# Long convolution of a two-layer kernel: a transform over 256 frequencies replaced by one over 128, with sums and differences on VectorE

## The reference

```python
def _bidir_long_conv(u, filt, bias):
    """y[t] = sum_s u[s] h(t - s) over offsets -(L-1)..(L-1), via FFT with zero padding to 2L. u: (B, L, C)."""
    l, ch = u.shape[1], u.shape[2]
    kern = jnp.concatenate([filt[:, :ch], jnp.zeros((1, ch), filt.dtype), filt[:0:-1, ch:]], axis=0)
    kern = kern * lax.rsqrt(jnp.sum(kern * kern, axis=0, keepdims=True))
    spec = jnp.fft.rfft(u, n=2 * l, axis=1) * jnp.fft.rfft(kern, axis=0)[None]
    y = jnp.fft.irfft(spec, n=2 * l, axis=1)[:, :l]
    return y + u * bias

def _hyena_mixer(p, ...):
    p = _short_conv(p.astype(f32), conv_w.astype(f32), conv_b.astype(f32))
    v, x1, x0 = jnp.split(p, 3, axis=-1)
    filt = _implicit_filter(...)
    return x0 * _bidir_long_conv(x1 * v, filt, bias.astype(f32))
```

## Time and profile before

| | |
|---|---|
| median of 3 runs | 3259.18 us |
| the profiled execution | 3258.49 us, span 3256.7 us |
| PE busy | 3151.7 us, 97% of the span |
| PEld busy | 2882.9 us, 89% |
| DVE busy | 1973.1 us, 61% |
| ACT busy | 1604.5 us, 49% |
| POOL busy | 2030.5 us, 62% |
| granted TensorE clock | 0.99 of full speed, mean |

### The profile page before, as it was taken

One profiled execution on the slowest core, in us unless ns is written; L12 is line 12 of the kernel. 1 busy time (PEld: TensorE's weight loads), 2 busy tenths in 40 slices (PEclk: granted clock), 3 DMA queues, 4 the chain that ended last, 5 costly groups with the idle time before them and its releaser, 6 DMA issues.

```text
span 3256.7 us, 59652 instructions
## 1 busy us (share of the span) xinstructions
PE 3151.7 (97%) x21316; PEld 2882.9 (89%) x21316; DVE 1973.1 (61%) x3192; ACT 1604.5 (49%) x2377; POOL 2030.5 (62%) x2676
## 2 busy tenths in 40 slices
PE   7999999999999999999998999999999999999998
PEld 7999999999888888888866989999987888888887
DVE  6566665666678766775866884555554443434344
ACT  6455554555454434444434665556554434444443
POOL 5777777777556655665643467888764555555553
PEclk9999999999999999999998999999999999999999
DMA  7676666666675575575545777676665555555553
GB/s 237 212 236 224 216 223 212 230 222 217 243 251 188 191 239 182 182 234 193 188 144 175 252 266 240 209 230 216 213 237 161 185 184 187 188 181 191 184 188 116
DMA packets 262849, 672.99 MB, mean 207 GB/s; under 512 B 28311, under 2 KB 65912, under 8 KB 262008
## 3 DMA queue, kind: packets, MB, share of 16 engines
q1 hardware_dynamic: 262584, 669.55, 62.6%
HBM read 663.12 MB, written 6.32 MB: 206 GB/s over the span
## 4 chain that ended last, share of the span: by engine, by line
PE 79%; POOL 8%; DVE 6%; issue 4%; DMA 2%; ACT 2%; SPq 0%; DVEq 0%; POOLq 0%; ACTq 0%
PE psum L768 30%; PE psum L769 15%; POOL w_lo L590 8%; PE psum L761 7%; PE psum L763 7%; PE psum L762 7%; PE psum L766 2%; PE psum L1820 1%; PE psum L1828 1%; PE psum L765 1%; DVE work L1051 1%; DVE psum L568 1%; DVE w_lo L590 1%; ACT w_hi L577 1%; PE psum L2353 1%
## 5 line engine op out<-in xcount | busy, mean ns | idle before, releaser
L590 POOL TENSOR_TENSOR w_lo<-raw,w_hi 128x256 fp32r<-128x256 f32 x2672 | 2030.3, 793 | 1203.7 <-ACT w_hi L577 1202.6
L577 ACT ACTIVATE w_hi<-raw 128x1024 fp32r<-128x1024 f32 (+3 forms) x1112 | 1050.1, 948 | 1185.1 <-PE psum L763 461.7
L768 PE MATMUL psum<-act_a,w_hi 128*128 128x512 f32 x2520 | 897.3, 399 | 2.1 <-DVE work L2145 1.3
L590 DVE TENSOR_TENSOR w_lo<-raw,w_hi 128x1024 fp32r<-128x1024 f32 (+2 forms) x332 | 425.7, 1282 | 491.0 <-ACT w_hi L577 490.6
L769 PE MATMUL psum<-act_a,w_lo 128*128 128x256 f32 x2520 | 707.6, 281 | 0.0
L768 PE MATMUL psum<-act_b,w_hi 128*128 128x512 f32 x1856 | 666.2, 401 | 6.6 <-DVE act_b L1041 5.4
L761 PE MATMUL psum<-act_a,w_lo 128*128 128x256 f32 x2016 | 595.3, 295 | 14.9 <-DVE act_a L1041 9.2
L768 PEld LDWEIGHTS psum<-act_a,w_hi 128*128 128x128 f32 x2520 | 473.5, 188 | 112.0 <-issue 2.0
L763 PE MATMUL psum<-act_a,w_hi 128*128 128x256 f32 x2016 | 572.3, 284 | 0.0
L762 PE MATMUL psum<-act_a,w_hi 128*128 128x256 f32 x2016 | 571.9, 284 | 0.0
L769 PE MATMUL psum<-act_b,w_lo 128*128 128x256 f32 x1856 | 522.6, 282 | 0.0
(11 more groups left out here) (383 smaller groups left out, 3665.2 us busy)
## 6 DMA issues: line engine op xcount, KB each, us to landing
raw<-w_mlp SPq DMA_DIRECT2D x256, 512.0 KB, 4.1
raw<-w_up SPq DMA_DIRECT2D x176, 512.0 KB, 3.6
raw<-w_dil SPq DMA_DIRECT2D x192, 384.0 KB, 3.5
work<-w_ada SPq DMA_DIRECT2D x288, 256.0 KB, 4.0
raw<-w_hg SPq DMA_DIRECT2D x128, 320.0 KB, 3.1
raw<-w_out SPq DMA_DIRECT2D x64, 512.0 KB, 5.2
raw<-w_down SPq DMA_DIRECT2D x64, 512.0 KB, 3.8
raw<-w_ada SPq DMA_DIRECT2D x128, 256.0 KB, 4.3
```

Source lines behind the costliest of these rows:

```text
L577: act.activation(w_hi[:, t % SPLIT, 0:nb * P], raw[:, t % RAW, 0:nb * P], ACT.Copy)\
L590: ins = eng.tensor_tensor(w_lo[:, t % SPLIT, cols], raw[:, t % RAW, cols], w_hi[:, t % SPLIT, cols], ALU.subtract)
L768: pe.matmul(bank, wh, src[:, kt, :], start=first, stop=False)
```

## The change

The transform of 256 tokens is split by even and odd tokens. Even tokens and odd tokens are each transformed for the lower 128 frequencies alone. The upper 128 follow from the same numbers with one sign turned: sum and difference of the two halves give the spectra at low and high frequencies. After the product with the filter's spectra, sums and differences give what the even and the odd tokens need, and each half is inverted from 128 frequencies. `dft` stays for the filter's own spectra, with its columns in the new order (high frequencies reversed, their sine part negated); `fold` and `unfold` (128x512 each) take the place of the transform and inverse tables of 128x1024 that the convolution loaded. `y_u` is stored with its even tokens first (L2614 after), and the gate at the end puts the tokens back in their order (L2653 after).

TensorE's transform becomes 4 matmuls of 128 columns in place of 8, and the inverse 4 matmuls of 128 columns in place of 4 of 256. VectorE's product grows from 6 instructions with one settle to 11 with four. None of the places at which the steps stand (the `yield`s) is changed.

```diff
--- before.py
+++ after.py
@@ -84,10 +84,12 @@
     k = (np.arange(S) + 0.5) * (2 * np.pi / (2 * S))
     ang = t[:, None] * k[None, :]
     cos, sin = np.cos(ang), np.sin(ang)
-    f = np.concatenate([cos, sin], 1)
+    low, high = slice(0, P), slice(S - 1, P - 1, -1)
+    f = np.concatenate([cos[:, low], cos[:, high], sin[:, low], -sin[:, high]], 1)
     c["dft"] = f.reshape(2, P, 2 * S).transpose(1, 0, 2).reshape(P, -1)
-    inv = np.stack([cos.T, sin.T], 0) / S
-    c["idft"] = inv.reshape(2, 2, P, S).transpose(2, 0, 1, 3).reshape(P, -1)
+    fold = np.stack([cos[:, low], sin[:, low]], 1).reshape(P, 2, 2, P)
+    c["fold"] = fold.reshape(P, -1)
+    c["unfold"] = (fold / S).transpose(3, 1, 2, 0).reshape(P, -1)
     names, cols, at = list(c), {}, 0
     for n in names:
         cols[n] = (at, c[n].shape[1])
@@ -2153,9 +2155,18 @@
 
         ar = Area(0)
         h_z, y_t = ar.take(5, S), ar.take(3, S)
-        dft, ld_dft = const(ar, "dft")
-        idft, ld_idft = const(ar, "idft")
+        fold, ld_fold = const(ar, "fold")
+        unfold, ld_unfold = const(ar, "unfold")
+        y_f = ar.take(4, P)
         assert ar.at <= KT * S
+
+        def by_parity(v):
+
+            return v.rearrange("p (m r) -> p r m", r=2)
+
+        def parities(v):
+
+            return v.rearrange("p (r m) -> p r m", r=2)
         ar = Area(two_base)
         y_par, h_gain = ar.take(NH, 13), ar.take(NH)
         h_reset, ld_reset = const(ar, "reset")
@@ -2578,7 +2589,8 @@
             return lambda columns: main, lambda columns: tail
 
 
-        yd = Chain("hy_dve_steps", per=14)
+        HY_STEPS = 19
+        yd = Chain("hy_dve_steps", per=HY_STEPS)
 
         def hy_dve(dve):
             ch = yd
@@ -2598,7 +2610,8 @@
                     yield
                 ch.step(dve.tensor_copy(y_c1[:, S - 1:S], y_c[1][:, S - 1:S]))
                 ch.settle()
-                dve.tensor_tensor(y_u, y_c[0], y_c1, ALU.mult).then_inc(sem("hy_u"), 1)
+                dve.tensor_tensor(parities(y_u), by_parity(y_c[0]), by_parity(y_c1), ALU.mult)\
+                   .then_inc(sem("hy_u"), 1)
                 yield
                 yield
                 yield
@@ -2610,14 +2623,23 @@
                 wait(dve, "hy_spec", i + 1)
                 wait(dve, "spec_loaded", i * 16 + 16)
                 u, f, y, w = A2(mix[:, 1, :], a=4), y_k, y_y, A2(mix[:, 2, :], a=4)
-                C, N = slice(0, 2), slice(2, 4)
-                ch.step(dve.tensor_tensor(y[:, C], u[:, C], f[:, C], ALU.mult))
-                ch.step(dve.tensor_tensor(w[:, C], u[:, N], f[:, N], ALU.mult))
-                ch.step(dve.tensor_tensor(y[:, N], u[:, C], f[:, N], ALU.mult))
-                ch.step(dve.tensor_tensor(w[:, N], u[:, N], f[:, C], ALU.mult))
+                C, N, LOW, HIGH = slice(0, 2), slice(2, 4), slice(0, 4, 2), slice(1, 4, 2)
+                ch.step(dve.tensor_copy(y[:, N], u[:, N]))
                 ch.settle()
-                dve.tensor_tensor(y[:, C], y[:, C], w[:, C], ALU.subtract)
-                dve.tensor_tensor(y[:, N], y[:, N], w[:, N], ALU.add).then_inc(sem("hy_prod"), 1)
+                ch.step(dve.tensor_tensor(y_f[:, LOW], u[:, C], y[:, N], ALU.add))
+                ch.step(dve.tensor_tensor(y_f[:, HIGH], u[:, C], y[:, N], ALU.subtract))
+                ch.settle()
+                ch.step(dve.tensor_tensor(y[:, C], y_f[:, C], f[:, C], ALU.mult))
+                ch.step(dve.tensor_tensor(w[:, C], y_f[:, N], f[:, N], ALU.mult))
+                ch.step(dve.tensor_tensor(y[:, N], y_f[:, C], f[:, N], ALU.mult))
+                ch.step(dve.tensor_tensor(w[:, N], y_f[:, N], f[:, C], ALU.mult))
+                ch.settle()
+                ch.step(dve.tensor_tensor(y[:, C], y[:, C], w[:, C], ALU.subtract))
+                ch.step(dve.tensor_tensor(y[:, N], y[:, N], w[:, N], ALU.add))
+                ch.settle()
+                dve.tensor_tensor(y_f[:, C], y[:, LOW], y[:, HIGH], ALU.add)
+                dve.tensor_tensor(y_f[:, N], y[:, LOW], y[:, HIGH], ALU.subtract)\
+                   .then_inc(sem("hy_prod"), 1)
                 yield
                 yield
                 yield
@@ -2628,7 +2650,8 @@
                 ch.step(dve.scalar_tensor_tensor(y_o, y_u, y_hp[:, 12:13], y_v,
                                                  ALU.mult, ALU.add))
                 ch.settle()
-                dve.tensor_tensor(y_v, y_o, y_c[2], ALU.mult).then_inc(sem("hy_out"), 1)
+                dve.tensor_tensor(by_parity(y_v), parities(y_o), by_parity(y_c[2]), ALU.mult)\
+                   .then_inc(sem("hy_out"), 1)
                 yield
                 yield
                 wait(dve, "pair_hi", i + LATER)
@@ -2673,18 +2696,16 @@
                 yield
                 wait(pe, "hy_uT_out", i + 1)
                 for m in range(4):
-                    for k in range(2):
-                        at = k * 2 * S + m * P
-                        ins = pe.matmul(mix[:, 1, m * P:(m + 1) * P], dft[:, at:at + P], y_uT[:, k, :],
-                                        start=(k == 0), stop=(k == 1))
+                    ins = pe.matmul(mix[:, 1, m * P:(m + 1) * P], fold[:, m * P:(m + 1) * P],
+                                    y_uT[:, m // 2, :], start=True, stop=True)
                 ins.then_inc(sem("hy_spec"), 1)
                 yield
                 yield
                 yield
                 wait(pe, "hy_prod", i + 1)
                 for m in range(4):
-                    ins = pe.matmul(mix[:, 2, 0:S], y_y[:, m, :], idft[:, m * S:(m + 1) * S],
-                                    start=(m == 0), stop=(m == 3))
+                    ins = pe.matmul(mix[:, 2, m // 2 * P:(m // 2 + 1) * P], y_f[:, m, :],
+                                    unfold[:, m * P:(m + 1) * P], start=(m % 2 == 0), stop=(m % 2 == 1))
                 ins.then_inc(sem("hy_back"), 1)
                 for _ in range(4):
                     yield
@@ -2752,7 +2773,7 @@
         FILTER = [ld_nf, (f_z[0:33], io["flt_z"]), (f_w1[0:33], io["flt_w1"]),
                   (f_w2[0:64], io["flt_w2"]), (f_w3[0:64], io["flt_w3"]),
                   (f_vec[0:64], io["flt_vec"]), (f_win.rearrange("p a b -> p (a b)"), io["flt_win"])]
-        TRANSFORMS, TRANSFORMS_AT = [ld_dft, ld_idft], (NH - 1, 2)
+        TRANSFORMS, TRANSFORMS_AT = [ld_fold, ld_unfold], (NH - 1, 2)
         TWO = [ld_reset, (y_par, io["hy_par"]), (h_gain, io["hg_gain"]),
                (h_mask.rearrange("p a b -> p (a b)").bitcast(I32), io["hg_mask"])]
         FILTER_LOADS, TWO_LOADS = len(FILTER) + 1, len(FILTER) + 1 + len(TRANSFORMS) + len(TWO)
@@ -3119,7 +3140,7 @@
             two_plan = two_mixers("pe", pe, hy_pe(pe), hg)
             phase(ph, act_b, two_plan, keep=True, carry=carried(plan, NH - 1, rate=1))
             meet(pe, "pe", "two_done")
-            last_rows = {NH - 1: ("hg_tail_steps", 6 * NH), KT - 1: ("hy_dve_steps", 14 * NH)}
+            last_rows = {NH - 1: ("hg_tail_steps", 6 * NH), KT - 1: ("hy_dve_steps", HY_STEPS * NH)}
             phase(PHD["out2"], act_a, hidden=lambda kt: last_rows.get(kt, ("hy_dve_steps", 0)), guard=("hy_uT_out", NH),
                   carry=carried(two_plan, NH - 1))
             meet(pe, "pe", "out2_done")
```

## The result

The changed kernel takes 3290.48 us (median of 4, 3284.27 to 3292.28); the kernel before takes 3259.47 us beside it. The ratio is 1.0089, 95% interval 1.0075 to 1.0103: slower by 31 us, where 14 were forecast. The direction was right and the size was not; 3290 lies above the range. The profiled execution took 3292.28 us, its span is 3290.5.

A forecast was written before the change was run, and what follows sets the result against it. The prediction took TensorE as the bound, busy 57.15 of a head's 58 us. Seven heads at +14.5 us and head 8 at -0.2 gave +14.3, so 3273 us, range 3264 to 3282.

The forecast's parts named there:

- What TensorE saves: Transform 0.91 us and inverse 0.73 us shorter, 1.64 us a head, 13.1 us over eight heads if nothing else moved.
- D: Length of VectorE's new product in a head, forecast at 6.4 us where the old product took 2.20 us.
- cover: Time between the product's end (L2620) and the inverse's start (L2686) before: 0.68 to 2.09 us, 10.10 over seven heads.
- 1.7 to 3.1 us a head: Idle time expected in the new profile ahead of the inverse (L2707), waiting for VectorE's L2641, in seven of eight heads.
- a head changes by D - 2.88 - cover: Heads 1 to 7: inverse starts D - 2.15 - cover later, is 0.73 us shorter; seven heads give +14.5 us.
- The product's length: VectorE's eleven instructions and four settles take 6.37 us, six two-SBUF ones slowed by GpSimd; bounds 4.24 and 7.5 us.
- Full exclusion: Rival, 10% together with a knock-on: each two-SBUF product instruction waits for a whole GpSimd piece, 0.95 us each; time 3284.
- the third rival: Part of a collision, 12%: GpSimd runs out of items, the product's last instructions run free; 5.3 us product, time near 3265.
- Cover and start: In seven heads the product starts behind the ada landing, not the transform, so the transform's 0.91 us is lost.
- head 8: In phase "out2" the product waits for the transform, starts 0.91 us earlier and takes 5.4 us: -0.2 us.
- What costs nothing: Strided operands at L2601 and L2631, ScalarE's and SyncE's waits for the product, and GpSimd's collision losses add no time.
- The range: Whole-kernel time from 3264 us (D = 5.1) to 3282 us (D = 7.5).

The follow-up runs named there:

- the kernel with that part alone: The kernel before with the change's smaller transform and inverse matmuls on TensorE, VectorE's old product kept: 3250.46 us against 3261.06.
- the change's two traces: The changed kernel profiled twice, unedited the second time: 3290.48 us, ratio 1.0089, then 3285.42 us, ratio 1.0061, against the kernel before.
- the earlier start: The change with VectorE's product one item earlier, ahead of the ada step: 3265.48 us against 3259.70 for the kernel before.
- the extra matmuls: The change with 12 unread TensorE matmuls ahead of the wait for the product in heads 1 to 7: 3281.00 us against 3259.70 before.
- the later inverse: The change with TensorE's inverse and VectorE's scale and gate one item later: 3280.84 us against 3263.41 for the kernel before.
- VectorE's part alone: The change with VectorE's eleven instructions but the old number and size of TensorE matmuls: 3294.16 us against 3261.06 for the kernel before.
- the 12-step kernel: The kernel before with twelve overwritten VectorE multiplications, each with a settle, added ahead of its product: 3312.38 us against 3261.06.

## Why the prediction was wrong

**What TensorE saves** was right as busy time: forecast 11.5 us in seven heads, measured 11.5 in the kernel with that part alone.

**The idle time** was right in sum. The prediction's terms put the inverse D - 2.15 - cover later and the transform 0.91 earlier: 7 x (6.4 - 1.24) - 10.10 = +26.0 us of idle time, against +26.2 and +29.2 measured. The sentence that TensorE would wait "1.7 to 3.1 us a head" was not what these terms give: with D = 6.4 it is 5.16 less the cover, 3.1 to 4.5 us and 3.7 on average. Measured: 2.81, 5.22, 3.66, 5.33, 2.81, 5.22 and 0.12 us, mean 3.6. That the sum agrees so well is partly luck. Heads 2, 4 and 6 waited 1.2 to 1.5 us longer than the terms give, and head 7 waited 3.3 us less: its product was 1.0 us shorter and began 0.6 us sooner after the transform than before, and TensorE came late to the wait because it had just worked at the lower clock. The sentence with "1.7 to 3.1" was a slip of working, and not harmless: it kept every pause well below the one of 3.97 us behind which the trace of before shows a low clock (below).

**The step that failed** is "a head changes by D - 2.88 - cover". It takes the work behind the pause to run as fast as before. It didn't: the granted clock fell to a half in the pauses of heads 1, 2, 4 and 6, just behind those of heads 3 and 5, and at the transform of head 7, and stayed there for some microseconds of work. The sum had no term for it, and the missing term measures 12.3 and 12.2 us. With it, 26.0 - 11.5 + 12.3 = 26.8 us for the stretch, where 27.1 was measured. The evidence was in the trace of before, on a row that I had used. The wait for GpSimd's L590 is given with a longest of 4.0 us. I read its total and not what came behind it. Timeline of PE before, at that pause:

```profile
1981.54 0.39 PE L761 MATMUL psum<-act_b,w_lo 128*128 128x256 f32 x1 [3.97 <-POOL w_lo L590]
...
1982.47 0.41 PE L762 MATMUL psum<-act_b,w_hi 128*128 128x256 f32 x1
1982.68 0.41 PE L763 MATMUL psum<-act_b,w_hi 128*128 128x256 f32 x1
```

and the windows there, before:

```profile
1982.50:1985.90 3.40, 3.40 (x19) 3.40 (x18) 1.28 (x3) 0.00 (x0) 3.40 (x5) 0.50 0.51 139
1986.50:1990.00 3.50, 3.50 (x31) 3.42 (x29) 0.00 (x0) 2.45 (x4) 3.50 (x6) 1.00 0.49 132
```

Behind the one pause of that length the grant is 0.50 for 3.4 us, and 19 records run in it where 31 run in 3.5 us behind it. They start 0.21 us apart instead of 0.12, so the work of 1.9 us took 3.4: an estimate of 1.5 us a pause. In seven heads with pauses of 3.1 to 4.5 us it would have added 10 us to the sum and put it at +25, time 3283. That is still short of the 12 us lost, since the low stretches behind the three pauses of over 5 us were 6.8 us long, in part inside the pauses. The pauses of at most 1.8 us for L2606 show a grant of 1.00 behind them. On this the Trainium skill ("TensorE: Matmul & The Clock Gate", section "HAM oscillation — how this bites in real kernels") says that a wait for DMA inside a loop can send the clock back to its low level each time round, so that the next work starts slow. The rows of heads 1 to 6 agree, with waits of 2.81 to 5.33 us for VectorE instead of a DMA.

**The product's length** was nearly right for the wrong mixture. Forecast 6.37 us; measured means 6.71 and 6.79. This groups view of DVE after, 2017 to 2424 us, gives busy us and mean ns over seven heads:

```profile
L2632 DVE TENSOR_TENSOR work<-work 128x256 f32<-128x256 f32 x7 | 13.2, 1891 | 0.2
L2635 DVE TENSOR_TENSOR psum<-work 128x256 f32<-128x256 f32 x7 | 4.8, 689 | 0.0
L2641 DVE TENSOR_TENSOR work<-work 128x256 f32<-128x256 f32 x7 | 4.8, 680 | 0.0
L2634 DVE TENSOR_TENSOR work<-work 128x256 f32<-128x256 f32 x7 | 4.5, 647 | 0.0
L2633 DVE TENSOR_TENSOR psum<-work 128x256 f32<-128x256 f32 x7 | 4.0, 575 | 0.0
...
L2640 DVE TENSOR_TENSOR work<-work 128x256 f32<-128x256 f32 x7 | 3.4, 480 | 0.2
```

34.7 us for 42 instructions is 0.83 each, inside the 0.7 to 0.95 forecast. But three of them, the first multiplications of heads 2, 4 and 6, hold 11.2 us (4.32, 3.45 and 3.45), and the other 39 average 0.60. Those three are also behind the three pauses of over 5 us. Full exclusion, one of the rivals, is not the answer either: it has 0.95 for each. Its time, 3284, came closer than mine, but not through its mechanism. What the third rival describes, GpSimd running out and the last instructions running free, did happen in heads 2, 4 and 6, but behind a first instruction that had waited for it, so these products became the longest and not the shortest.

**Cover and start** were right: the product started behind the ada landing, 2.8 to 4.5 us after the transform. So was head 8 in size: its product started 1.09 us after the transform (forecast 1.07) and took 5.71 us (5.4), which makes about +0.1 instead of -0.2 us.

**What costs nothing** held in the change, where ScalarE's wait for the product hid behind TensorE's, but only there: with the inverse an item later it shows as 9.6 us. **The range** took its bounds from D alone. Its upper end, D = 7.5, was not reached by the mean of any trace with this product; a range that follows from one unknown can't hold a term that is absent.

What stays open: why the change's whole-run medians differ (31.0 and 22.0 us above before's) while its stretches differ by 3 us the other way; the intervals overlap. And how the remaining cost splits between long waits and turns in runs other than the traced ones.

## What to carry to other kernels

When a new wait will stop TensorE for more than some 2 us, look in the trace of before for a pause as long, read the granted clock where the work resumes, and give it a term of its own. Here it was worth 12 us beside 26 of idle time. Price a link of a relay by its latency and its place, not by the engine's share of busy time: the same arithmetic with one operand in PSUM and a start one item earlier turned +31 us into -8.6. And when a forecast gives an idle time per head, work it out from the same terms as the sum.

## What the hardware showed unexpectedly

A VectorE instruction with both inputs in SBUF did not always wait for one GpSimd piece. Beside GpSimd pieces of 0.60 us it took 0.42 to 0.99 us in most cases, but 2.68 to 4.93 us in twelve products: three each in the change's two traces (4.32, 3.45, 3.45 and 4.29, 3.94, 2.99 us), one with the earlier start, three with the extra matmuls and two with the later inverse. It was always the first multiplication, and it always ended about 0.28 us after GpSimd's last piece, with GpSimd then idle for 5.9 to 7.9 us: VectorE got in only when GpSimd had run out of work. VectorE's part alone had none in eight. On this the Trainium skill ("SBUF — State Buffer", section "Who interferes with whom") says that the later of the two engines is blocked for the other's instruction. Both patterns differ from that. GpSimd's pieces of 128x256 took 0.73 us on average in the undisturbed run of the earlier trace rows and 0.88 beside VectorE, so a turn cost GpSimd less than a whole VectorE instruction; and the long waits span five to eight pieces. What decides between the two patterns was not found.

The clock: the pauses before the inverse up to 2.2 us were never followed by a lower grant, those of 2.22 to 2.93 us in seven of twelve cases, those above 3.2 us always in these traces (3.14 us in head 1 of the 12-step kernel was not). At other places shorter waits were followed by one too: 1.83, 1.95 and 2.15 us at the transform of head 7 in three traces and 1.84 us at L2535 with the later inverse, while waits of 2.0 to 2.2 us at the transform of other heads were not. So no length of a pause separates the cases. The grant fell to a half each time, and in the change came to 34 us at 1.2 GHz, for which 12 us were lost.
